# Last expert's rows added by a one-hot matmul, the other pairs loaded meanwhile, experts' rows copied by ScalarE

## The reference, cut to what matters

```python
for l in range(DEPTH):                                  # DEPTH = 2
    ...
    h = modulate(rmsnorm(x, norm2_g[l]), sh2, sc2)
    x = x + g2[:, None, :] * moe(h, ...)                # g2: one row of 1024, from the condition c
return rmsnorm(x, final_g)

def moe(h, ...):                                        # 16 experts, each token goes to 2 of them
    expert_idx, weights = route(h, w_router, b_router)
    # per expert: (silu(x @ w_gate) * (x @ w_up)) @ w_down
    # per token: the sum of its two rows, each times its weight
```

## Time and profile before

| | us |
|---|---|
| median of 3 runs | 1528.97 |
| lowest, highest | 1526.42, 1530.14 |
| the profiled execution's own time | 1528.16 |
| its span, from the first to the last instruction | 1526.3 |
| TensorE (PE) busy | 1451.0 (95%) |
| VectorE (DVE) busy | 1115.2 (73%) |
| ScalarE (ACT) busy | 771.4 (51%) |
| GpSimd (POOL) busy | 117.2 (8%) |
| share of the chain of work that ended last | TensorE 81%, VectorE 10%, issue 3%, ScalarE 3%, DMA 2% |

### The profile page before, as it was taken

One profiled execution on the slowest core, in us unless ns is written; L12 is line 12 of the kernel. 1 busy time (PEld: TensorE's weight loads), 2 busy tenths in 40 slices (PEclk: granted clock), 3 DMA queues, 4 the chain that ended last, 5 costly groups with the idle time before them and its releaser, 6 DMA issues.

```text
span 1526.3 us, 18846 instructions
## 1 busy us (share of the span) xinstructions
PE 1451.0 (95%) x6878; PEld 1159.2 (76%) x6878; DVE 1115.2 (73%) x1487; ACT 771.4 (51%) x1100; POOL 117.2 (8%) x141
## 2 busy tenths in 40 slices
PE   6999999999999999999869999999999999999991
PEld 1778888778878787777658888878887877777771
DVE  4584566465668999999968556754346899999995
ACT  3333433323346777777723434241234577777772
POOL 0000001000002111110000000100000111111000
PEclk9999999999999999999979999999999999999996
DMA  9566165454557999999776533632253789999985
GB/s 380 213 207 195 42 199 198 144 186 160 189 207 245 368 368 384 372 383 366 275 282 208 193 111 111 209 123 97 83 202 128 286 290 371 383 372 379 364 336 191
DMA packets 106499, 373.96 MB, mean 245 GB/s; under 512 B 16603, under 2 KB 16795, under 8 KB 105636
## 3 DMA queue, kind: packets, MB, share of 16 engines
q1 hardware_dynamic: 88512, 323.00, 59.0%
q0 software_dynamic: 15552, 41.30, 7.5%
q10 hardware_dynamic: 2340, 8.42, 1.4%
HBM read 357.42 MB, written 31.50 MB: 255 GB/s over the span
## 4 chain that ended last, share of the span: by engine, by line
PE 81%; DVE 10%; issue 3%; ACT 3%; DMA 2%; DVEq 1%; ACTq 0%; SPq 0%; POOLq 0%
PE ps L1462 24%; PE ps L1464 23%; PE ps L1463 23%; DVE w_lo L1279 5%; ACT w_hi L711 2%; PE ps L1551 2%; PE ps L1693 2%; DVE y_out L1300 1%; PE ps L1765 1%; PE ps L1614 1%; DMA raw<-w 1%; PE ps L1672 1%; PE ps L1618 1%; PE ps L1659 1%; PE ps L1597 1%
## 5 line engine op out<-in xcount | busy, mean ns | idle before, releaser
L1279 DVE TENSOR_TENSOR w_lo<-raw,w_hi 128x1024 fp32r<-128x1024 f32 x360 | 426.6, 1220 | 13.7 <-ACT w_hi L711 13.7
L711 ACT ACTIVATE w_hi<-raw 128x1024 fp32r<-128x1024 f32 x360 | 367.5, 1056 | 27.3 <-PE ps L1464 27.2
L861 DVE TENSOR_TENSOR w_lo<-raw,w_hi 128x1024 fp32r<-128x1024 f32 x136 | 165.9, 1224 | 229.1 <-ACT w_hi L544 227.6
L544 ACT ACTIVATE w_hi<-raw 128x1024 fp32r<-128x1024 f32 x136 | 142.8, 1057 | 339.8 <-PE ps L1464 338.3
L1462 PE MATMUL ps<-w_hi,hT_lo 128*128 128x512 f32 x576 | 231.0, 401 | 3.0 <-DVE hT_lo L942 3.0
L1464 PE MATMUL ps<-w_hi,hT_hi 128*128 128x512 f32 x576 | 225.5, 392 | 0.0
L1463 PE MATMUL ps<-w_lo,hT_hi 128*128 128x512 f32 x576 | 225.3, 391 | 0.0
L1462 PE MATMUL ps<-w_hi,xgT_lo 128*128 128x512 f32 x512 | 206.4, 403 | 4.1 <-DVE w_lo L861 1.4
L1464 PE MATMUL ps<-w_hi,xgT_hi 128*128 128x512 f32 x512 | 200.2, 391 | 0.0
L1463 PE MATMUL ps<-w_lo,xgT_hi 128*128 128x512 f32 x512 | 199.7, 390 | 0.0
L1462 PEld LDWEIGHTS ps<-w_hi,hT_lo 128*128 128x128 f32 x576 | 108.7, 189 | 29.8 <-DVE hT_lo L942 4.1
(11 more groups left out here) (244 smaller groups left out, 2020.4 us busy)
## 6 DMA issues: line engine op xcount, KB each, us to landing
raw<-w SPq DMA_DIRECT2D x592, 512.0 KB, 5.6
h_rows<-h POOLq DMA_DIRECT2D x8, 1024.0 KB, 5.3
ahead<-w SPq DMA_DIRECT2D x4, 2048.0 KB, 10.6
y_pair<-y_rows ACTq DMA_DIRECT2D x8, 1024.0 KB, 8.7
x_state<-x POOLq DMA_DIRECT2D x2, 2048.0 KB, 7.5
x<-x_state POOLq DMA_DIRECT2D x4, 1024.0 KB, 7.6
x<-x_in SPq DMA_DIRECT2D x4, 512.0 KB, 11.3
gate_row<-mod_rows POOLq DMA_DIRECT2D x4, 512.0 KB, 6.4
```

Source lines behind the costliest of these rows:

```text
L544: act.activation(w_hi[:, q % W_SLOTS], raw[:, r % RAW_SLOTS], ACT.Copy).then_inc(w_hi_ready, 1)
L711: act.activation(w_hi[:, n % W_SLOTS], expert_piece(e, n), ACT.Copy).then_inc(w_hi_ready, 1)
L861: v.tensor_tensor(w_lo[:, q % W_SLOTS], raw[:, r % RAW_SLOTS], w_hi[:, q % W_SLOTS], ALU.subtract).then_inc(raw_used, 1)
L1279: v.tensor_tensor(w_lo[:, n % W_SLOTS], expert_piece(e, n), w_hi[:, n % W_SLOTS], ALU.subtract).then_inc(raw_used, 1)
```

## The change

The last expert's rows are no longer stored and loaded again. VectorE builds a one-hot matrix with the tokens' weights (`last_hot`), TensorE turns it and multiplies it by the last expert's `y_out`, into two PSUM banks per tile of tokens, and VectorE adds the banks to `x` (`last_add`). The pairs are loaded by SP's queue as soon as the rows of experts 0 to 14 are stored; weights of slots that belong to the last expert are zero (`w_early`), and `y_rows` is filled once from `x_in`, so that no slot is unwritten. Tiles 0 and 1 are loaded into the region of `hT`. ScalarE scales the first row of a pair (`scale_pair`), VectorE adds the second row, multiplies by the gate row and adds to `x`. Experts 0 to 14 leave their PSUM banks by two ScalarE copies without the gate; only the last expert's are multiplied by VectorE. The order of VectorE's work at both ends changes, and the splits of the next layer's first four pieces stand among it.

```diff
@@ SyncE @@
+            def pairs_load(l):
+
+                for p in range(2):
+                    sp.wait_ge(row_stored[p], (l + 1) * STORED[p])
+                for t in range(2):
+                    sp.dma_start(pair_early[:, t], y_tiles[t]).then_inc(pair_in[t], 16)
+                sp.dma_start(pair_2[:], y_tiles[2]).then_inc(pair_in[2], 16)
+                for j in range(2):
+                    sp.dma_start(pair_3[j][:], y_tiles[3][:, j]).then_inc(pair_in[3], 16)
...
                     if l and r == W_SLOTS:
-                        for t in range(NT):
-                            sp.wait_ge(pair_in[t], l * 16)
+                        pairs_load(l - 1)
...
+            pairs_load(DEPTH - 1)
@@ ScalarE @@
                 if name == "u":
+                    if l == 0:
+                        for t in range(NT):
+                            act.dma_start(y_tiles[t], x_in[:, t * D:(t + 1) * D].unsqueeze(1).broadcast_to([P, 2, D])
+                                          ).then_inc(y_filled, 16)
...
+                def rows_out(before):
+
+                    act.wait_ge(w_used, l * PROD + (MIX + EXP * before + EXP + W_SLOTS))
+                    act.wait_ge(row_stored[before % 2], l * STORED[before % 2] + (before // 2) * 16 + 32)
+                    for half in range(2):
+                        one = act.activation(y_out[:, before % 2, 512 * half:512 * half + 512], ps[:, 2 + half], ACT.Copy)
+                    one.then_inc(y_copied, 1)
+
+                if e:
+                    rows_out(e - 1)
                 hi_e(4)
                 hi_e(5)
...
+                else:
+                    scale_pair(l, 0)
+                    scale_pair(l, 1)
+
+            def scale_pair(l, t):
+
+                act.wait_ge(pair_in[t], (l + 1) * PAIR_DMAS[t])
+                act.activation(pair(t, 0), pair(t, 0), ACT.Copy, scale=w_early[:, t:t + 1]).then_inc(pair_scaled, 1)
...
                 act.activation(spare[:], k("eps"), ACT.Sqrt)
                 if l < DEPTH - 1:
-                    for q in range(W_SLOTS):
+                    for q in range(W_SLOTS - 1):
                         hi(l + 1, q, RAW_OF_W[q])
-                for p in range(2):
-                    act.wait_ge(row_stored[p], l * 160 + 160)
-                apart(act)
-                for t in range(NT):
-                    act.dma_start(y_pair[:, t], y_tiles[t]).then_inc(pair_in[t], 16)
-                apart(act)
+                scale_pair(l, 2)
+                act.wait_ge(hot_last_turned, l + 1)
+                act.activation(slot_last[:], ps[:, 4].rearrange("p (a b) -> p a b", a=NT), ACT.Copy).then_inc(slot_last_ready, 1)
+                scale_pair(l, 3)
+                if l < DEPTH - 1:
+                    hi(l + 1, W_SLOTS - 1, RAW_OF_W[W_SLOTS - 1])
@@ VectorE @@
                 one.then_inc(hot_ready, 1)
+                pair_weights()
...
+            def pair_weights():
+
+                v.tensor_scalar(w_slots[:], posk[:], float(CAP), None, ALU.is_lt)
+                v.drain()
+                tt(w_slots[:], w_slots[:], wts[:], ALU.mult)
+                tt(w_both[:].unsqueeze(2), w_slots[:].unsqueeze(2),
+                   hots[:].rearrange("p (s e) -> p s e", e=NE)[:, :, NE - 1:NE], ALU.mult)
+                v.tensor_tensor(w_early[:], w_slots[:], w_both[:], ALU.subtract)
+                tt(w_last[:], w_both[:, 0:4], w_both[:, 4:8], ALU.add)
+
+            def last_hot(l):
+
+                for t in range(NT):
+                    at_last = NE * t + NE - 1
+                    one = v.tensor_scalar(hot_last[:, t], k("iota"), pos[:, at_last:at_last + 1], w_last[:, t:t + 1],
+                                          ALU.is_equal, ALU.mult)
+                one.then_inc(hot_last_ready, 1)
...
                 lo_e(4)
                 lo_e(5)
-                if e:
-                    rows_out(e - 1, 0)
                 hidden(0)
                 lo_e(6)
-                if e:
-                    rows_out(e - 1, 1)
                 lo_e(7)
...
                 if last:
+                    last_hot(l)
+                    for t in range(2):
+                        combine(l, t)
                     rows_out(e, 0)
                     rows_out(e, 1)
...
             def combine(l, t, parts=(0, 1)):
 
                 if 0 in parts:
-                    v.wait_ge(pair_in[t], l * 16 + 16)
-                    v.scalar_tensor_tensor(x[:, t], y_pair[:, t, 0], wts[:, t:t + 1], x[:, t], ALU.mult, ALU.add)
+                    v.wait_ge(pair_scaled, l * NT + (t + 1))
+                    v.scalar_tensor_tensor(pair(t, 1), pair(t, 1), w_early[:, 4 + t:5 + t], pair(t, 0), ALU.mult, ALU.add)
                     v.drain()
                 if 1 in parts:
-                    v.scalar_tensor_tensor(x[:, t], y_pair[:, t, 1], wts[:, 4 + t:5 + t], x[:, t], ALU.mult,
-                                           ALU.add).then_inc(x_final, 1)
+                    v.tensor_tensor(pair(t, 1), pair(t, 1), gate_row[:], ALU.mult)
+                    v.drain()
+                    v.tensor_tensor(x[:, t], x[:, t], pair(t, 1), ALU.add)
+                    v.drain()
+
+            def last_add(l, t):
+
+                v.wait_ge(last_added, l * NT + (t + 1))
+                v.tensor_tensor(x[:, t].rearrange("p (h n) -> p h n", h=2), ps[:, ADD_BANK[t]:ADD_BANK[t] + 2],
+                                x[:, t].rearrange("p (h n) -> p h n", h=2), ALU.add).then_inc(x_final, 1)
...
-                    combine(l - 1, 0)
-                    combine(l - 1, 1, (0,))
+                    lo(l, 0, RAW_OF_W[0])
+                    last_add(l - 1, 0)
+                    last_add(l - 1, 1)
                     norm_tile(l, 0, "h1", 0)
-                    combine(l - 1, 1, (1,))
+                    lo(l, 1, RAW_OF_W[1])
+                    lo(l, 2, RAW_OF_W[2])
                     norm_lo(l, "h1", 0)
-                    for t in range(1, NT):
-                        norm_tile(l, 0, "h1", t)
-                        if t + 1 < NT:
-                            combine(l - 1, t + 1)
-                        norm_lo(l, "h1", t)
+                    lo(l, 3, RAW_OF_W[3])
+                    combine(l - 1, 2)
+                    norm_tile(l, 0, "h1", 1)
+                    last_add(l - 1, 2)
+                    norm_lo(l, "h1", 1)
+                    combine(l - 1, 3)
+                    norm_tile(l, 0, "h1", 2)
+                    last_add(l - 1, 3)
+                    norm_lo(l, "h1", 2)
+                    norm_tile(l, 0, "h1", 3)
+                    norm_lo(l, "h1", 3)
...
-                if l < DEPTH - 1:
-                    for q in range(W_SLOTS):
-                        lo(l + 1, q, RAW_OF_W[q])
-                v.nop()
-
-            for t in range(NT + 1):
-                if t < NT:
-                    combine(DEPTH - 1, t)
-                if t:
-                    normed_output(t - 1)
+            last = DEPTH - 1
+            combine(last, 2)
+            last_add(last, 0)
+            last_add(last, 1)
+            combine(last, 3, (0,))
+            normed_output(0)
+            combine(last, 3, (1,))
+            last_add(last, 2)
+            normed_output(1)
+            last_add(last, 3)
+            normed_output(2)
+            normed_output(3)
@@ TensorE, after the last expert @@
+            def last_rows_added(l):
+
+                pe.wait_ge(hot_last_ready, l + 1)
+                for t in range(NT):
+                    one = pe.transpose(ps[:, 4, t * P:(t + 1) * P], hot_last[:, t], ident)
+                one.then_inc(hot_last_turned, 1)
+                pe.wait_ge(slot_last_ready, l + 1)
+                pe.wait_ge(z_half, l + 1)
+                for t in range(NT):
+                    for half in range(2):
+                        if t == 0 and half == 1:
+                            pe.wait_ge(y_copied, l * NE + (NE + 1))
+                        one = pe.matmul(ps[:, ADD_BANK[t] + half], slot_last[:, t], y_out[:, (NE - 1) % 2, 512 * half:512 * half + 512],
+                                        start=True, stop=True)
+                    one.then_inc(last_added, 1)
@@ GpSimd @@
                     gather(l, e + XG_SLOTS)
+                if e == NE - 1:
+                    return
                 pool.wait_ge(y_copied, E + 2)
+                if E == 0:
+                    pool.wait_ge(y_filled, 16 * NT)
```

More of the change, by code:

```diff
@@ L222, in build @@
         hidT_lo = sb("hidT_lo", [P, 512], F32R, A + 28672)
-        y_pair = sb("y_pair", [P, NT, 2, D], F32, A)
+        pair_early = sb("pair_early", [P, 2, 2, D], F32, hT_at)
+        pair_2 = sb("pair_2", [P, 2, D], F32, A)
+        pair_3 = [sb(f"pair_3{j}", [P, D], F32, A + 8192 + 8192 * j) for j in range(2)]
+        hot_last = sb("hot_last", [P, NT, P], F32, A + 30720)
+        slot_last = sb("slot_last", [P, NT, P], F32, A + 24576)
         cond_wide = sb("cond_wide", [P, 8, 32], F32, A)
@@ L312, in build @@
         wts = small("wts", 8)
```

(42 more changed lines are left out.)

29 lines of the change are left out of this document (22 added, 7 removed).

## The result

| us | before | after |
|---|---|---|
| median of 20 runs each | 1528.67 | 1531.54 |
| lowest, highest | 1526.25, 1530.99 | 1528.32, 1534.07 |
| profiled execution, its span | 1528.16, 1526.3 | 1533.05, 1531.2 |

The ratio of after to before is 1.0020, interval 1.0014 to 1.0026: 2.9 us slower, clear of the noise of 20 runs, and within the 0.3% that the prediction called no change. The experts got shorter, and the boundary between the layers took back more than they gave.

A forecast was written before the change was run, and what follows sets the result against it. The kernel was taken as a TensorE stream with holes, inside experts and at layer ends. Experts -8.4, first layer's end +9.4 and end +0.9 gave +1.9 us: 1531 us forecast, range 1520 to 1540.

The forecast's parts named there:

- experts, 30 x 0.28: Experts 1 to 15 of two layers: lighter VectorE shortens each by 0.28 us, 8.4 us in all; bounds 0 to 12.9.
- first layer's end: Boundary between the layers: sums, y_out, adding matmuls and norms come later, costing 9.4 us; least 6, most 12.5.
- end: End of the kernel: same order of sums and adding matmuls costs 0.9 us; between -1 and 2.
- small additions: Weight operations and four row-buffer issues (about 2 us) hide in waits, costing nothing; uncovered, 1.4 us twice and 2 once.
- Rows copied by ScalarE: In each expert: VectorE loses two instructions, 1.2 us; ScalarE's two copies, 1.1 us, cost nothing; gain 0.28 us.
- the cover before the silu: In each expert: ScalarE's 1.62 us idle before its silu holds the 1.1 us of copies with 0.5 to spare.
- now at the full clock: Layer 1's first products, after the half-clock adding matmuls, start at 782.1 against 778.15 and run at full clock.
- The rival of a second fall: Clock falls again while TensorE waits about 5 us for tile 1; up to 4 us more, 1535 us; chance 0.1.
- about 5 and 3 us of TensorE idle: Sign of being right: TensorE idles this long in layer 1's first group, each wait ending with a normalized tile.
- The transfer rate: The skill's 358 GB/s would keep experts from shortening, sum +10.3; the trace's 406 and 382 GB/s disagreed.

The follow-up runs named there:

- e1_copies: Kernel before, with ScalarE copying the output rows of experts 0 to 14 and their gate left out; sums as before: 1521.06 us, ratio 0.995.
- e7_gate_in_sums: Kernel before, with ScalarE copying all experts' rows and the gate multiplied in the tile sums; no one-hot product, no early loads: 1532.78 us, ratio 1.0027.
- e5: Changed kernel, with products without a use keeping TensorE busy while it waits for expert 15's rows and before tile 0's transposes: 1529.01 us, ratio 1.0006.
- e6: Changed kernel, with TensorE adding each tile's first pair, ScalarE copying expert 15's rows, and three VectorE passes a tile: 1526.53 us, ratio 0.9991.
- e3: Changed kernel, with VectorE reading all experts' rows and multiplying by the gate there, no gate in the tile sums: 1537.35 us, ratio 1.0061.
- e8: Changed kernel rebuilt: gate in VectorE's reads, expert 15's rows first, TensorE adding first pairs, one VectorE pass waiting only for the pair: 1516.64 us, ratio 0.9917.
- e4: Changed kernel, with expert 15's rows and the one-hot copies ahead of the sums, and tile 0 normed before tile 1: 1528.06 us, ratio 0.9998.

## Why the prediction was right

1531.0 us was forecast and 1531.54 measured, as no change within 0.3%. The path was the predicted one; that the number came within 0.6 us is in part luck, since 1.9 us were forecast and the medians are 2.9 apart and the two profiles 4.9. The sum against the profiles:

| step | predicted | measured |
|---|---|---|
| experts, 30 x 0.28 | -8.4 | -4.1 and -3.6 = -7.7 |
| first layer's end | +9.4 | +11.6 |
| end | +0.9 | +0.4 |
| small additions | 0 | +0.7 up to the routing |

*Rows copied by ScalarE.* Right in place and size: 17.97 us, 0.26 less, and the cover before the silu held. e1_copies shows it alone. That this half is undone by the gate's place is what e7_gate_in_sums adds.

*Small additions.* The issues that fill the row buffer took ScalarE 3.85 us, not about 2, and it began the state at 161.85 instead of 161.10:

```profile
157.96 3.85 ACTq L695 DMA_DIRECT2D y_rows<-x_in  x4
161.85 1.03 ACT L637 ACTIVATE state<-kv_sum 128x256 f32<-128x256 f32 x3 [3.30 <-DVE kv_sum L1068]
```

It can cost time where the cover is too short. TensorE waits for that state in after, and in before it doesn't:

```profile
162.32 0.70 PE L1735 MATMUL ps<-state,qT 128*128 128x256 f32 x2 [0.46 <-ACT state L637]
```

The four issues take from 2.9 to 4.9 us, from one profile to the next. In e5 and e6 they took 2.92 and 2.95, nobody waited, and the routing was reached at 444.95 and 444.75, sooner than before (445.46). In e3, e8 and e4 they took 4.26, 4.17 and 4.85, and TensorE waited 0.88, 0.78 and 1.47. So the working had put at nothing a term of 0 to 1.5 us a run, 0.46 in after's profile. The rest of what varies up to the routing stays open.

*The first layer's end.* The working has a slip in its last sum: 805.6 + 0.9 + 6 x 1.37 is 814.7, not 815.1, so its own terms give 9.0 and not 9.4. The chain went as predicted: y_out behind two sums, the adding matmuls at half clock, then VectorE leading tile by tile. Counted from the start of the last product, the adding matmuls start 11.9 us later (predicted 10.2), tile 0 is normalized 21.6 later (21.5), tile 1 32.9 (32.8), tile 2 43.0 (42.3), tile 3 49.7 (48.6). That tile 0 fits so well is luck: two terms were off against each other. Tile 0's pairs came 1.9 us later than put (ScalarE's scaling starts at 755.36), and the clock came back after 4 us of work, not 8 (windows of 1 us; the third number from the end is the granted clock, before the DMA share and GB/s):

```profile
759.00:760.00 1.00, 0.00 (x0) 0.00 (x0) 0.93 (x2) 0.98 (x2) 0.00 (x0) 0.63 1.04 414
...
769.00:770.00 1.00, 1.00 (x3) 0.47 (x2) 0.81 (x1) 0.00 (x0) 0.00 (x0) 0.75 0.57 221
770.00:771.00 1.00, 1.00 (x4) 0.44 (x3) 0.41 (x1) 0.55 (x1) 0.00 (x0) 1.00 0.00 0
...
780.00:781.00 1.00, 1.00 (x4) 0.81 (x3) 0.93 (x2) 0.00 (x0) 0.00 (x0) 0.50 0.81 266
...
788.00:789.00 1.00, 1.00 (x5) 0.81 (x4) 0.69 (x1) 0.74 (x3) 0.00 (x0) 0.50 0.00 0
...
798.00:799.00 1.00, 1.00 (x5) 0.81 (x4) 0.79 (x2) 0.75 (x3) 0.83 (x2) 0.50 0.00 0
```

What remains, 2.2 us, lies in the term that was mis-sized: the step took the products "now at the full clock". The clock fell three more times, in short stretches near 780, 788 and 798. Tiles 1 and 2 were turned in 1.90 and 1.73 us instead of 1.06; how much of the 1.1 us that tile 3's norm is late comes from it is not shown. In the last stretch the turn of tile 2 and the six products behind it took 3.93 us, where e5's at the full clock take 2.31. So TensorE was not done with tile 2 when tile 3 was ready at 803.2; it turned it at 804.55, 1.35 late. The rival of a second fall named this, with a price of up to 4 and a wait of 5 us as its cause; it came behind waits of 2.36, 3.25 and 1.86 us. The sign "about 5 and 3 us of TensorE idle" was off with it: these waits are 3.25 and 1.86, since products at half the clock filled the rest. With TensorE kept busy (e5) the boundary is 57.6, 9.0 over before. That is near the predicted 9.4, but not the predicted case, which had the adding matmuls at half the clock where e5 has them at the full one.

*The end.* Right: last_add 0 at 1511.97, a wait of 1.11 for tile 1 (1.5 predicted), 0.4 in all.

*The transfer rate.* Experts did get shorter, at 385 GB/s in the window above. The Trainium skill (DMA: Bandwidth & Descriptors, Where 436 GB/s comes from) says that transfers between HBM and SBUF bind at some 358 GB/s; the trace still doesn't agree.

What the working didn't see is that 9.4 was not the price of the idea. It came from order (5.8 us in e4), from the gate's passes (2.4 where they stood, in e3) and from the clock (2.6 in e5, not all of it); these overlap and can't be summed.

## What to carry to other kernels

An operation moved off a busy engine has to be paid where it lands. The gate came with VectorE's reads of the rows, two of 0.69 us per expert; once ScalarE did the reading, it became a pass of its own of 1.23 us for each tile, at the ends of the layers, where part of it lay open. When a round trip through memory is replaced by work on engines, count what else VectorE does in that time: from the last split the trip of before took 13.4 us to the first sum, with four splits of the next layer beside it; the chain that replaced it took 18.5 us until the last rows could be added to tile 0. Put what another engine waits for (here expert 15's rows and the turned one-hots) ahead of what only you wait for, and look for the second thing it waits for before moving the first. Test the same edit separately at each place where it occurs: here the one-hot product won 7.5 us at the end and lost 7.8 at the boundary.

## What the hardware showed beyond that

Beside GpSimd's multiplication of two SBUF operands (3.5 us for 128x1024) one of VectorE's subtractions took 3.42 us instead of 1.22, the one that followed the subtraction running when GpSimd began; its neighbours kept their length. TensorE's clock fell not only in the wait of 11 us, but also around waits of 3.25, 2.36, 1.86 and, in three profiles, 1.1 to 1.2 us; in others the same 1.1 us went by without a fall. Products without a use, in the wait of 11 us and ahead of tile 0's turn, made the kernel 2.1 to 2.5 us shorter. Four issues of the same DMA took ScalarE's queue from 2.9 to 4.9 us.
